# Sums of squares in four column groups, a root along the free dimension, and its table loaded ahead

## The reference

```python
def rmsnorm(x, g):
    xf = x.astype(jnp.float32)
    y = xf * lax.rsqrt(jnp.mean(xf * xf, axis=-1, keepdims=True) + EPS)
    return (y * g.astype(jnp.float32)).astype(x.dtype)

def swiglu(h, w_in, w_out):
    gate, up = jnp.split(h @ w_in, 2, axis=-1)
    return (jax.nn.silu(gate) * up) @ w_out
```

## Time and profile before

| | |
|---|---|
| median of 3 runs | 2319.43 us (2317.01 to 2323.76) |
| span of the profiled execution | 2321.3 us; what lies around it isn't listed |
| PE busy | 2129.8 us, 92% |
| VectorE, ScalarE, POOL busy | 1004.5, 797.4, 704.5 us |
| mean granted clock of PE | 0.947 of full speed |
| sums of squares L451 | 456 records, 64.9 us busy |
| table loads for the roots of L479 and L550 | 8, each 1.283 us |

### The profile page before, as it was taken

How to read it: one execution, slowest core, us unless ns; L and a number is a source line. 1 busy time by engine, 2 the same in 40 slices (tenths; PEclk the granted TensorE clock), 3 DMA queues, 4 the chain that set the end, 5 groups by cost and what they waited for, 6 DMA issues and landing times.

```text
span 2321.3 us, 27177 instructions
## 1 busy us (share of the span) xinstructions
PE 2129.8 (92%) x9966; PEld 1711.8 (74%) x9966; DVE 1004.5 (43%) x1613; ACT 797.4 (34%) x1160; POOL 704.5 (30%) x297
## 2 busy tenths in 40 slices
PE   2889989858899999989999999989999998999998
PEld 2668766647678888878888877755777877888887
DVE  4676888694323220142322034665667323222201
ACT  2222134532334342144433223445333324344312
POOL 0222210120244444424444433320310342444442
PEclk8889999876999999999999999989979999999999
DMA  8668730201122222222222232200210121222221
GB/s 314 227 236 276 252 125 1 91 9 37 64 93 97 99 92 98 90 100 93 97 99 90 100 110 78 81 35 12 73 37 1 67 88 64 99 99 90 100 90 64
DMA packets 63290, 230.38 MB, mean 99 GB/s; under 512 B 7024, under 2 KB 7280, under 8 KB 62704
## 3 DMA queue, kind: packets, MB, share of 16 engines
q1 hardware_dynamic: 62928, 229.03, 28.1%
q10 hardware_dynamic: 288, 0.33, 0.0%
HBM read 227.24 MB, written 2.10 MB: 99 GB/s over the span
## 4 chain that ended last, share of the span: by engine, by line
PE 68%; DVE 13%; issue 6%; DMA 6%; ACT 3%; POOL 2%; SPq 0%; DVEq 0%; ACTq 0%; POOLq 0%
PE ps L364 57%; DMA raw<-stream 6%; DVE raw L407 3%; POOL w_lo L1400 2%; ACT prob L856 1%; PE ps L1920 1%; PE ps L451 1%; PE ps L1900 1%; PE ps L1901 1%; PE ps L1789 1%; PE ps L1769 1%; DVE prob L902 1%; ACT w_hi L376 1%; DVE t L510 1%; PE ps L1009 1%
## 5 line engine op out<-in xcount | busy, mean ns | idle before, releaser
L1400 POOL TENSOR_TENSOR w_lo<-raw,w_hi 128x1024 fp32r<-128x1024 f32 x284 | 684.2, 2410 | 1502.4 <-ACT w_hi L376 863.3
L364 PE MATMUL ps<-hh,w_hi 128*128 128x512 f32 (+1 forms) x1576 | 634.5, 403 | 46.6 <-POOL w_lo L1400 29.2
L364 PE MATMUL ps<-hl,w_hi 128*128 128x512 f32 (+1 forms) x1576 | 626.2, 397 | 0.0
L364 PE MATMUL ps<-hh,w_lo 128*128 128x512 f32 (+1 forms) x1576 | 625.5, 397 | 0.0
L364 PEld LDWEIGHTS ps<-hh,w_hi 128*128 128x128 f32 (+1 forms) x1576 | 302.9, 192 | 125.2 <-POOL w_lo L1400 33.0
L364 PEld LDWEIGHTS ps<-hh,w_lo 128*128 128x128 f32 (+1 forms) x1576 | 302.8, 192 | 66.1
L364 PEld LDWEIGHTS ps<-hl,w_hi 128*128 128x128 f32 (+1 forms) x1576 | 303.5, 193 | 62.2
L1425 DVE TENSOR_TENSOR prod<-silu,ps 128x512 f32<-128x512 f32 x66 | 45.4, 688 | 457.7 <-PE ps L364 436.5
L1381 ACT ACTIVATE w_hi<-raw 128x1024 fp32r<-128x1024 f32 x132 | 140.1, 1062 | 299.0 <-PE ps L364 298.6
L407 DVE SCALAR_TENSOR_TENSOR raw<-raw,cond_ada 128x1024 f32<-128x1024 f32 x72 | 123.5, 1745 | 234.9 <-DMA raw<-stream 234.5
L364 PE MATMUL ps<-act_hi,w_hi 128*128 (+1 forms) x528 | 208.7, 395 | 0.0
(11 more groups left out here) (383 smaller groups left out, 2521.2 us busy)
## 6 DMA issues: line engine op xcount, KB each, us to landing
raw<-stream SPq DMA_DIRECT2D x420, 512.0 KB, 3.3
xT<-xT SPq DMA_DIRECT2D x2, 1024.0 KB, 12.4
out<-fin SPq DMA_DIRECT2D x8, 256.0 KB, 2.0
csta<-csta SPq DMA_DIRECT2D x1, 1344.0 KB, 18.7
cT<-cT SPq DMA_DIRECT2D x1, 1024.0 KB, 16.0
cond<-cond SPq DMA_DIRECT2D x1, 512.0 KB, 6.8
cond_ctx<-cond_ctx SPq DMA_DIRECT2D x1, 512.0 KB, 7.8
cond_ada<-cond SPq DMA_DIRECT2D x1, 512.0 KB, 14.0
```

The costliest lines, as they stand in the source:

```text
L364: mm = pe.matmul(out, w, r, start=first and i == 0, stop=last and i == 2)
L1400: pool.tensor_tensor(w_lo[g % SPLIT][:, :], raw[n % RING][:, :], w_hi[g % SPLIT][:, :].bitcast(F32), ALU.subtract)\
```

## The change

Squares are now the moving operand, and 32 columns of ones the weights: the sums of token tile t lie on partitions 32t to 32t + 31, tokens along 128 columns. The root and the reciprocal work on these 128 columns (64 partitions for the context) in one of two buffers `row_root`. The spread takes as weights the column of the identity that picks partition 32t. A root of one number (`root_ahead`) stands ahead of the squares of each norm, and draws the table load there. In the feed-forwards five of the eight sums move into the last slab, three chunks behind; the sums go to bank 0 and the spread to bank 1. In the head norms a root waits until the spread before the last has read its buffer.

```diff
@@ -138,9 +138,10 @@
     half_gate = {n: sb(f"half_gate_{n}", [P, KD]) for n in ("f1", "f2")}
     std = {}
     rs = {}
-    for n, w in (("nx", NT), ("nc", NTC), ("nq", 32), ("nk", 48), ("no", 16), ("ng", 16), ("n2", NT), ("nf1", NT),
-                 ("nm", NT), ("ncq", NT), ("nckv", NT), ("nf2", NT), ("nfin", NT)):
+    for n, w in (("nq", 32), ("nk", 48)):
         std[n], rs[n] = sb(f"std_{n}", [P, w]), sb(f"rs_{n}", [P, w])
+    row_root = [sb(f"row_root{i}", [P, P]) for i in range(2)]
+    root_first = sb("root_first", [P, 1])
     lam = sb("lam", [P, 8])
     gain_dn = sb("gain_dn", [P, 1])
     gain_dq = sb("gain_dq", [P, 1])
@@ -441,28 +442,36 @@
 
         return S("norm_" + what), norm_base[key][what] + count
 
+    def tile_sums(pe, b, squares, tokens, first, last):
+
+        for t in range(tokens // P):
+            mm = pe.matmul(ps[32 * t:32 * t + 32, b, 0:P], c("one").broadcast_to([P, 32]), squares[:, t * P:(t + 1) * P],
+                           start=first, stop=last)
+        return mm
+
+    def tile_spread(pe, b, root, tokens):
+
+        for t in range(tokens // P):
+            mm = pe.matmul(ps[:, b, t * P:(t + 1) * P], c("ident", 32 * t, 32 * t + 1).broadcast_to([P, P])[0:32 * (tokens // P), :],
+                           root[0:32 * (tokens // P), :], start=True, stop=True)
+        return mm
+
     def norm_sum(pe, key, k, chunks, tokens, ba):
 
         if k == 0:
             norm_starts(key, chunks)
             claim(pe, ba, key + "_ss")
         pe.wait_ge(*norm(key, "sq", k + 1))
-        for t in range(tokens // P):
-            mm = pe.matmul(ps[:, ba, t * P:(t + 1) * P], sq[k % 2][:, t * P:(t + 1) * P], c("one").broadcast_to([P, P]),
-                           start=(k == 0 and t == 0), stop=(k == chunks - 1), skip_group_check=True)
+        mm = tile_sums(pe, ba, sq[k % 2], tokens, k == 0, k == chunks - 1)
         mm.then_inc(S("norm_sq_used") if k < chunks - 1 else bank_full(ba), 1)
 
     def norm_tensor(pe, key, chunks, tokens, ba, bb, first=0):
 
-        tiles = tokens // P
         for k in range(first, chunks):
             norm_sum(pe, key, k, chunks, tokens, ba)
         claim(pe, bb, key + "_rs", norm(key, "t1", chunks))
         pe.wait_ge(*norm(key, "rs", 1))
-        for t in range(tiles):
-            mm = pe.matmul(ps[:, bb, t * P:(t + 1) * P], rs[key][:, t:t + 1].broadcast_to([P, P]), ident,
-                           start=True, stop=True)
-        mm.then_inc(bank_full(bb), 1)
+        tile_spread(pe, bb, row_root[norm_base[key]["rs"] % 2], tokens).then_inc(bank_full(bb), 1)
 
     def norm_square(act, key, src, k, tokens, ready):
         ready(act, k)
@@ -470,13 +479,20 @@
             act.wait_ge(*norm(key, "sq_used", k - 1))
         act.activation(sq[k % 2][:, 0:tokens], src[:, k, :], ACT.Square).then_inc(S("norm_sq"), 1)
 
+    def root_ahead(act):
+
+        act.activation(root_first[:, :], c("eps"), ACT.Sqrt)
+
     def norm_scalar(act, key, src, chunks, tokens, width, hi, shift, ready, meanwhile=None):
 
         if ready is not None:
+            root_ahead(act)
             for k in range(chunks):
                 norm_square(act, key, src, k, tokens, ready)
         b = full(act, key + "_ss")
-        act.activation(std[key][:, :], ps[:, b, 0:tokens:P], ACT.Sqrt, bias=c("eps"), scale=1.0 / width).then_inc(bank_empty(b), 1)
+        rows = slice(0, 32 * (tokens // P))
+        act.activation(row_root[norm_base[key]["rs"] % 2][rows, :], ps[rows, b, 0:P], ACT.Sqrt, bias=c("eps")[rows, :],
+                       scale=1.0 / width).then_inc(bank_empty(b), 1)
         if hi is None:
             return
         if meanwhile is not None:
@@ -490,7 +506,8 @@
 
     def norm_vector(dve, key, src, chunks, tokens, gains, hi, lo, shift, out=None):
         read(dve, key + "_ss")
-        dve.reciprocal(rs[key][:, :], std[key][:, :]).then_inc(S("norm_rs"), 1)
+        rows, i = slice(0, 32 * (tokens // P)), norm_base[key]["rs"] % 2
+        dve.reciprocal(row_root[i][rows, :], row_root[i][rows, :]).then_inc(S("norm_rs"), 1)
         b = full(dve, key + "_rs")
 
         def low(k):
@@ -524,21 +541,16 @@
 
         claim(pe, b, (key + "_ss", h))
         pe.wait_ge(*norm(key, "sq", h + 1))
-        for t in range(NT):
-            mm = pe.matmul(ps[:, b, t * P:(t + 1) * P], sq[h % 2][:, t * P:(t + 1) * P], c("one").broadcast_to([P, P]),
-                           start=True, stop=True)
-        mm.then_inc(bank_full(b), 1)
+        tile_sums(pe, b, sq[h % 2], N, True, True).then_inc(bank_full(b), 1)
 
     def head_spread(pe, key, h, b):
         claim(pe, b, (key, h), norm(key, "t1", h + 1))
         pe.wait_ge(*norm(key, "rs", h + 1))
-        for t in range(NT):
-            mm = pe.matmul(ps[:, b, t * P:(t + 1) * P], rs[key][:, h * NT + t:h * NT + t + 1].broadcast_to([P, P]),
-                           ident, start=True, stop=True)
-        mm.then_inc(bank_full(b), 1)
+        tile_spread(pe, b, row_root[(norm_base[key]["rs"] + h) % 2], N).then_inc(bank_full(b), 1)
 
     def head_norm_scalar(act, key, src, chunk0, ready, final, meanwhile=None):
 
+        root_ahead(act)
         for turn in range(HEADS + 2):
             h = turn
             if h < HEADS:
@@ -547,7 +559,9 @@
             h = turn - 1
             if 0 <= h < HEADS:
                 b = full(act, (key + "_ss", h))
-                act.activation(std[key][:, h * NT:(h + 1) * NT], ps[:, b, 0:N:P], ACT.Sqrt, bias=c("eps"), scale=1.0 / DV)\
+                if h >= 2:
+                    full(act, (key, h - 2))
+                act.activation(row_root[(norm_base[key]["rs"] + h) % 2][:, :], ps[:, b, 0:P], ACT.Sqrt, bias=c("eps"), scale=1.0 / DV)\
                    .then_inc(bank_empty(b), 1)
             h = turn - 2
             if 0 <= h < HEADS:
@@ -564,8 +578,8 @@
 
         for h in range(HEADS):
             read(dve, (key + "_ss", h))
-            cols = slice(h * NT, (h + 1) * NT)
-            dve.reciprocal(rs[key][:, cols], std[key][:, cols]).then_inc(S("norm_rs"), 1)
+            i = (norm_base[key]["rs"] + h) % 2
+            dve.reciprocal(row_root[i][:, :], row_root[i][:, :]).then_inc(S("norm_rs"), 1)
             b = full(dve, (key, h))
             if h >= 2:
                 dve.wait_ge(*norm(key, "ready", h - 1))
@@ -1223,6 +1237,7 @@
 
 
     SUM_LAG = 2
+    FFN_LAG = 3
     RESIDUALS = ("mix1_diff", "mix1", "ffn1", "ffn2", "mix2", "ffn3")
 
     def residual(key, chunks):
@@ -1293,7 +1310,7 @@
     ffns = {}
     HALF = KF // 2
 
-    def ffn_tensor(pe, key, key_norm, name_in, name_out):
+    def ffn_tensor(pe, key, key_norm, name_in, name_out, sums_of):
         f = ffns[key] = dict(i=len(ffns), n0=len(stream), g0=len(slot_of))
         for b in range(4):
             pe.wait_ge(*bank_freed[b])
@@ -1352,6 +1369,8 @@
                 mm = three_passes(pe, ps[:, m, :], g, m, P, act_hi[:, act_at], act_lo[:, act_at], first, last)
                 if last:
                     mm.then_inc(bank_full(m), 1)
+                    if m >= FFN_LAG:
+                        norm_sum(pe, sums_of, m - FFN_LAG, KD, N, 0)
             if not last:
                 mm.then_inc(S("slab_done"), 1)
 
@@ -2152,10 +2171,10 @@
             new_slot(half_slots(pair, 0))
         half_mixed_tensor(pe, "mix1", 0, firsts["mix1"], 0, "ng", "n2")
         norm_tensor(pe, "n2", KD, N, 4, 5, KD - SUM_LAG)
-        ffn_tensor(pe, "ffn1", "n2", "w_ffn_in", "w_ffn_out")
-        norm_tensor(pe, "nf1", KD, N, 4, 5)
-        ffn_tensor(pe, "ffn2", "nf1", "w_ffn1_in_2", "w_ffn1_down_2")
-        norm_tensor(pe, "nm", KD, N, 4, 5)
+        ffn_tensor(pe, "ffn1", "n2", "w_ffn_in", "w_ffn_out", "nf1")
+        norm_tensor(pe, "nf1", KD, N, 0, 1, KD - FFN_LAG)
+        ffn_tensor(pe, "ffn2", "nf1", "w_ffn1_in_2", "w_ffn1_down_2", "nm")
+        norm_tensor(pe, "nm", KD, N, 0, 1, KD - FFN_LAG)
         proj2_tensor(pe)
         lora_tensor(pe)
         mla_tensor(pe)
@@ -2165,8 +2184,8 @@
         firsts["mix2"] = len(slot_of)
         mixed_tensor(pe, "mix2", "w_out_2", yh, yl, [(S("y_ready"), k + 1) for k in range(KD)], "nf2")
         norm_tensor(pe, "nf2", KD, N, 4, 5, KD - SUM_LAG)
-        ffn_tensor(pe, "ffn3", "nf2", "w_ffn2_in_2", "w_ffn2_down_2")
-        norm_tensor(pe, "nfin", KD, N, 4, 5)
+        ffn_tensor(pe, "ffn3", "nf2", "w_ffn2_in_2", "w_ffn2_down_2", "nfin")
+        norm_tensor(pe, "nfin", KD, N, 0, 1, KD - FFN_LAG)
 
     @block.scalar
     def _(act):
```

## The result

| | before | changed |
|---|---|---|
| median | 2321.60 us, 4 runs (2317.01 to 2324.58) | 2339.3 us, 4 runs (2336.52 to 2343.61) |
| span of the profiled execution | 2321.3 us | 2336.0 us |
| mean granted clock of PE | 0.947 | 0.941 |
| sums of squares, head norms included | 520 records (L451, L528), 74.7 us | 520 records (L448), 31.3 us |

The ratio is 1.0077, 95% interval 1.0055 to 1.0100. The prediction was 2322 (2315 to 2330): wrong, and outside its range. The sums keep PE busy for 43 us less (L451's 456 records took 64.9 us, the 64 of the head norms' L528 9.8), and the kernel is 15 to 18 us slower.

What follows compares the result with a forecast made beforehand. The prediction took the chain of waits, 68% PE, as the bound, with the change's worth in the norm gaps. Its terms summed to +1.1 us, plus 2.0 for the clock: +3.1 on 2319.43, so 2322.5, predicted 2322, range 2315 to 2330.

Steps and rivals of the forecast that it cites:

- The wait for bank 1: Between nf1 and ffn2: ffn2's first matmul waits until VectorE's last product of the norm frees bank 1; +7.9 us.
- the first rival: Whole kernel: the gain comes after all, with sums at 0.42 us and no clock fall in the tails; 2315, chance 0.15.
- nf1's tail: Last slab of ffn1: PE stands 3.5 us for square 0, so moving the sums gains nothing; +0.3 us.
- Head norms +1.0: The two head norms: longer reciprocals on VectorE's path, partly returned by cheaper sums; +1.0 us for both, between 0 and 3.
- a spread at the low clock perhaps: Clock allowance: pauses in ffn1's and ffn2's last slabs, perhaps one norm's spread at 2.06 us; +2.0 us, between 0 and 9.
- The ends of the mixes: Ends of mix1 and mix2: the last sum waits for its square, giving back what root and reciprocal take; +0.2 us for both.
- The mixes' sums: Twelve sums between matmuls in mix1 and mix2: each costs 0.55 us instead of 0.89; -4.1 us.
- nfin: End of ffn3: no weight to fetch, m = 3 needs no wait, so the spread starts earlier; -2.8 us.
- ncq and nckv: These two norms: table load and small root first, then squares, one sum, root, reciprocal; -1.3 us each, -2.6 together.
- nx and nc: Norm nx and the context's norm nc: VectorE's longer reciprocal stands on the path; +0.75 us each, +1.5 together.
- the clock decides against it: Last slabs of ffn1 and ffn2: the clock falls to half during the wait for square 0; +8.5 us, 2329, chance 0.12.
- The third rival: All sums: column groups run one after the other, 1.2 us a sum, +15.6 us; 2338, chance 0.08.

Runs made afterwards that it cites:

- e1: The changed kernel with the spreads of nf1, nm and nfin back in bank 5; 2331.5 us, ratio to before 1.0038.
- e8: e1 with table load and small root of nf1, nm and nfin before each feed-forward's last weight copy; 2326.88 us, ratio to before 1.0034.
- e2: The changed kernel with no sums in the last ffn slabs: all eight behind in bank 4, spread in bank 5; 2326.63 us, ratio to before 1.0030.
- e5: e2 plus unused matmuls on PE at n2, nf1, nm, nf2 and nfin; 2316.41 us, ratio to before 0.9978.
- e3: The kernel before with only the tail edit: ffn sums in the last slab, spread in bank 1, old forms kept; 2330.62 us, ratio 1.0036.
- e6: The kernel before plus unused matmuls (two and eight) at n2, nf1, nm, nf2 and nfin; 2321.56 us, ratio 0.9998.
- e11: e7 plus idle matmuls before the last two head spreads of no and ng, and at ncq and nckv; 2316.06 us, ratio to before 0.9977.
- e13: e7 plus six idle matmuls before the spreads of the last two heads of no and ng; 2314.88 us, ratio to before 0.9975.
- e7: e5 with the head norms in old form and the table load and small root before each ffn's last weight copy; 2313.01 us, ratio to before 0.9967.

## Why the prediction was wrong

- **The wait for bank 1: right.** Place, releaser and size were as written: +7.9 predicted, 7.8 in e1's time, 8.1 in the stretch. The 2.3 us for the low clock, in this term and in the first rival's sum, is an estimate that no run shows as such. In its place the runs show PE's first 12 matmuls behind the wait taking 5.21 us, from 1023.03 to 1028.24, at a granted 0.50: 2.4 more than 12 x 0.2325. Before, with no such wait, they took 5.26 (1006.76 to 1012.02), so the term rests on the later start alone, 1014.6 for 1006.76 in the prediction's numbers.
- **nf1's tail: place right, size low.** The order of steps is as written (wait of 3.58 for square 0, 3.5 predicted). The tail without the bank's wait costs 2.4 (e1), for +0.3 and a share of the clock of 1.0. The low clock at chunk 5 cost 1.4 of it (e8 against e1), and the changed kernel's spread took 1.78. All told the tail edit cost 12.7 in the time (e2 against the changed kernel); the sum had 7.1 for the three tails, the new form's gain included.
- **"Head norms +1.0": this term failed most.** They cost 6. The 0.5 for ng was right as arithmetic (19.4 for 18.9 in e8); the 4.7 that came on top are half clock through all of ng (granted 0.50 until 598). The norm no took part too: from its first spread to its fourth 10.9 and 10.6 us in two executions of the changed kernel, 9.0 before, with the fourth spread at 2.05. The sum gave the clock 2.0 us, "a spread at the low clock perhaps", and looked for it in the tails only. The earlier trace rows had shown a spread at 2.06 us, nx's, at a granted 0.50, and the earlier trace rows nf1's at 1.13: the sign that a norm of this kernel can meet either level.
- **The ends of the mixes, "+0.2 for both": failed for the same reason.** The mixes' sums are worth what was predicted: residuals with a sum come 6.16 us apart (1908.80, 1914.96) for 6.47, so a sum costs 0.56 (0.55 predicted), 0.31 saved twelve times, 3.7 us. In mix2, from 1880.63 to the last residual, 1.5 was gained, and from there to steady ffn3 1.9 lost, with the spread at 2.05 and ffn3's first matmuls at half rate; e5 takes that back.
- **nfin: number right by luck, reason wrong.** 2.8 nearer, as predicted, but e2 has it without the move (359.8 from steady to spread; after 360.3, before 363.1). The last residual, the last square and one sum stand behind the slab either way; what was saved is the queue of long sums. The root's spread then ran at the low clock (2.04 us, granted 0.50 from 2326) and gave 0.9 back.
- **ncq and nckv: not shown.** The stretch is 2.8 shorter, but so it is in e3, which has the old form there (141.9 us; after 141.8, before 144.6), and it isn't in the changed kernel's second execution (144.6). The number fits by chance. What repeats is 0.8 us at nckv: from ncq's spread to nckv's 9.07 us in both executions of the changed kernel, 9.83 before, for the 1.3 predicted.
- **nx and nc: not on the path for long.** Of +1.5, 0.1 is left at 322 us, where projections wait for the weights (on the chain of before a landing of 3.49 us from 294.60).
- **Rivals.** The one closest to what happened is "the clock decides against it", named with 0.12 and placed in the ffn tails. There it came true for one or two chunks of four; for the rest the clock decided in ng, at n2, nf2 and nfin. The third rival's 2338 is nearest in number by luck: serial column groups are excluded, with eight records in 0.42 us. A sum between other matmuls, out and back included, costs 0.56 us.

The step that failed, in one sentence: the sum priced each stretch outside the ffn tails at the clock it had before and put 2.0 us in all for the clock, though the change took PE's work out of the very stretches beside which rows of before show the half clock; measured were 4.7 us in ng alone, and 10 us at n2, nf1, nm, nf2 and nfin in the new form (e2 against e5).

## What to carry to other kernels

Work taken from PE in the gaps where another engine set the pace gained nothing here, and it cost the clock of what followed: ng took 24.1 us for 18.9, and five norms lost 10 us (e2 against e5). Before such a change, mark every place within some us of which the granted clock is already below 1, and price it at both levels. Matmuls that nobody reads, put where PE only waits, gave 10 us in the new form (e5); in the old form (e6) and in the head norms (e11, e13) the time showed nothing of them. When a result moves to another bank, look up what later code waits for on that bank: this one line of arguments cost 8 us, and nothing in the diff spoke of it.

## What the runs showed of the hardware

- Four column groups of 32, fp32, full height: eight records start and end within 0.42 us, where eight of the old form take 0.98; sixteen in a row take 0.64. Between other matmuls the price is 0.56 us, of which the 0.22 of eight more records is less than half. The rest lies at its two ends (e8, from 993.35): the first record starts 0.32 and not 0.23 behind the last matmul, the next matmul 0.36 behind the first record, and the one after it 0.34 and not 0.23 later.
- VectorE's reciprocal goes on at 6.2 ns a column up to 128: 948 to 953 ns, after 178, 347 and 444 ns at 4, 32 and 48.
- The same program can go through the same gap at either clock: e7's ng took 23.2 and 18.9 us in two executions. A profile of one execution can be 4 us off at one norm by that alone, and the profiled executions of e8 and e13 lie 8.5 and 5.5 us under the medians of their kernels.
